# Down matrices asked for by the ScalarEngine, gate and up matrices by the SyncEngine, in a two-layer trunk with 64 experts a layer

## The reference

```python
def hier_moe(x, w_grp, b_grp, w_exp, b_exp, w_gate, w_up, w_down):
    # top-1 expert group of 8, then top-2 of its 8 experts; 64 experts in all
    ...
    def run_block(args):
        tok, e = args
        xb = x_pad[tok]
        h = jax.nn.silu(xb @ w_gate[e]) * (xb @ w_up[e])
        return h @ w_down[e]
    ...
    y = jnp.sum(y_assign.reshape(T, TOP_K, D).astype(jnp.float32) * weights[..., None], axis=1)
```

## Time and profile before

| | |
|---|---|
| median of 3 runs | 1505.33 us (1503.81 to 1505.48) |
| profiled execution, device time | 1503.91 us |
| its span | 1502.2 us |
| PE busy | 1259.2 us (84%) |
| DVE, ACT busy | 554.2 us (37%), 207.2 us (14%) |
| chain that ended last | PE 60%, DMA 36% |
| of that, transfers of `in_w_down` into `scratch` | 35% |
| matmuls of L1497 (down), in the chain | 11% |
| DMA queue q1 (SyncE) | 501.84 MB, 83.3% of 16 engines |
| DMA queue q10 (ScalarE) | 1.06 MB, 0.2% |

### The profile page before, as it was taken

The page is one execution under the profiler, slowest core; times in us unless marked ns, Lnnn a source line. Parts: engine busy times, 40 slices in busy tenths (PEclk is TensorE's granted clock), DMA queues, the critical chain, the costliest instruction groups (busy, mean ns, idle before and its releaser), DMA issues.

```text
span 1502.2 us, 20998 instructions
## 1 busy us (share of the span) xinstructions
PE 1259.2 (84%) x8621; PEld 690.0 (46%) x8621; DVE 554.2 (37%) x987; ACT 207.2 (14%) x413; POOL 27.9 (2%) x90
## 2 busy tenths in 40 slices
PE   9999999986774777579999999999677568757797
PEld 5665444742342434235466554456334325423354
DVE  6677775510110111111667677754111101101126
ACT  2322000310100000000212220012111000000011
POOL 2000000000000000000100000000000000000000
PEclk9999999997888889889999999999888879888899
DMA  9644558899999999999955255679999999999992
GB/s 314 230 172 150 174 211 332 318 426 426 427 427 425 425 425 426 428 427 416 330 192 204 97 204 168 230 301 355 426 427 426 427 426 424 426 426 428 426 408 87
DMA packets 110537, 503.85 MB, mean 335 GB/s; under 512 B 13042, under 2 KB 16132, under 8 KB 62468
## 3 DMA queue, kind: packets, MB, share of 16 engines
q1 hardware_dynamic: 109876, 501.84, 83.3%
q10 hardware_dynamic: 592, 1.06, 0.2%
HBM read 501.83 MB, written 1.05 MB: 335 GB/s over the span
## 4 chain that ended last, share of the span: by engine, by line
PE 60%; DMA 36%; issue 1%; SPq 1%; DVE 1%; ACT 0%; POOL 0%; DVEq 0%; POOLq 0%
DMA scratch<-in_w_down 35%; PE ps L852 20%; PE ps L1497 11%; PE ps L901 6%; PE ps L1448 5%; PE ps L805 4%; PE ps L1429 2%; PE ps L1507 2%; PE ps L1615 1%; PE ps L1344 1%; PE ps L825 1%; SPq L553 1%; PE ps L1316 0%; DMA ring<-in_w_in 0%; PE ps L1367 0%
## 5 line engine op out<-in xcount | busy, mean ns | idle before, releaser
L1497 PE MATMUL ps<-ring,pads 128*32 128x512 f32 x384 | 161.6, 784 | 199.2 <-DMA scratch<-in_w_down 199.2
L1497 PEld LDWEIGHTS ps<-ring,pads 128*32 128x32 f32 x384 | 33.9, 139 | 300.6 <-DMA scratch<-in_w_down 162.3
L1448 PE MATMUL ps<-scratch,pads 128*32 128x256 f32 x1792 | 171.6, 379 | 0.0
L1448 PE MATMUL ps<-ring,pads 128*32 128x256 f32 x2304 | 171.4, 379 | 0.0
L852 PE MATMUL ps<-ring,scratch 128*128 128x512 f32 x384 | 169.2, 592 | 0.0
L1497 PE MATMUL ps<-scratch,pads 128*32 128x512 f32 x512 | 161.6, 790 | 0.0
L2657 DVE COPY mats<-ps 128x512 f32<-128x512 f32 x32 | 22.1, 691 | 349.3 <-PE ps L1497 349.3
L1429 PEld LDWEIGHTS ps<-pads,xT 128*128 128x128 f32 x960 | 114.8, 197 | 25.3 <-issue 25.3
L1429 PE MATMUL ps<-pads,xT 128*128 128x128 f32 x960 | 116.0, 280 | 10.6 <-issue 10.6
L1507 PE MATMUL ps<-mats,pads 128*128 128x512 f32 x256 | 118.8, 606 | 0.0
L1448 PEld LDWEIGHTS ps<-scratch,pads 128*32 128x32 f32 x1792 | 89.3, 110 | 58.9 <-issue 17.6
(11 more groups left out here) (364 smaller groups left out, 1314.3 us busy)
## 6 DMA issues: line engine op xcount, KB each, us to landing
ring<-in_w_up SPq DMA_DIRECT2D x28, 2048.0 KB, 32.5
scratch<-in_w_down SPq DMA_DIRECT2D x28, 2048.0 KB, 23.0
scratch<-in_w_gate SPq DMA_DIRECT2D x28, 2048.0 KB, 30.4
ring<-in_w_in SPq DMA_DIRECT2D x48, 1024.0 KB, 7.1
ring<-in_w_gate SPq DMA_DIRECT2D x12, 3072.0 KB, 31.8
scratch<-in_w_up SPq DMA_DIRECT2D x14, 2048.0 KB, 31.9
ring<-in_w_down SPq DMA_DIRECT2D x14, 2048.0 KB, 27.0
scratch<-in_w_gate SPq DMA_DIRECT2D x22, 1024.0 KB, 14.5
```

Source lines behind the costliest of these rows:

```text
L1448: ins = mm(ps[32 * j:32 * j + 32, 2, i * 256:i * 256 + 256], xgT[:, k, 32 * j:32 * j + 32], w[j][:, k, :], start=(k == 0), stop=(k == K - 1))
L1497: ins = mm(ps[32 * j:32 * j + 32, n, :], hT[:, cc, 32 * j:32 * j + 32], w[j][:, cc, n * 512:n * 512 + 512], start=(cc == 0), stop=(cc == 1 ...
```

## The change

The high down matrices of most groups, and the low ones two groups ahead, are asked for by ScalarE: behind `take_down` of a turn it waits for `down_read` and issues high(s+1) and low(s+2). `down_read` is a new semaphore that PE raises with the second matmul of gate(s+1), that is, one matmul after the `ring_free` step that SyncE waited for before. SyncE keeps all gate and up matrices, the down matrices of groups 0 and 15, and around the sections' border low(1), low(8), high(8) and low(9). The slots and their order of reuse are as before. ScalarE's loop over turns now takes two groups a turn of the loop, and the last turns are written out.

```diff
@@ gate_up (TensorE)
+                                if i == 0 and k == 0 and j == 1 and not first:
+                                    ins.then_inc(down_read, 1)
@@ SyncE
                     with sp.Fori(first, PAIRS) as g:
                         for uu in range(2):
                             load_part(m + uu, GATE_UP, g)
-                            load_part(m + uu - 1, DOWN_HI, g)
-                            load_part(m + uu, DOWN_LO, g)
...
                 load_part(MID, DOWN_LO)
-                load_pairs(MID + 1)
-                load_part(GROUPS - 1, GATE)
-                load_part(GROUPS - 2, DOWN_HI)
-                load_part(GROUPS - 1, UP)
+                load_part(MID + 1, GATE_UP)
+                load_part(MID, DOWN_HI)
+                load_part(MID + 1, DOWN_LO)
+                load_part(MID + 2, GATE_UP)
+                load_pairs(MID + 1, 1)
+                load_part(GROUPS - 1, GATE_UP)
@@ ScalarE
+                def load_down(m, n, turn, g=None):
+
+                    act.wait_ge(down_read, turn)
+                    alone(act)
+                    s = m if m < MID else m + OVERG
+                    for n0, n1 in [run for run in PLAN[L]["runs"][s % 2] if n <= run[0] < n + 2]:
+                        q, e = MOE0 + 12 * s + n0, L * NE + 4 * m + n0 - 8
+                        src = a["w_down"][bass.ds(e if g is None else g * 8 + e, n1 - n0), :, :]
+                        act.dma_start(run_ap(PLAN[L]["slots"][q:q + n1 - n0]), src.rearrange("e (p k) n -> p e (k n)", k=2)).then_inc(
+                            landed[leader_of(L, s, n0)], 16)
...
+                    with act.Fori(0, pairs) as g:
+                        for uu in range(2):
+                            turn(g * 2 + (c0 + uu + 1))
+                            load_down(m0 + uu + 1, 10, g * 2 + (turns + uu + 1), g)
+                            load_down(m0 + uu + 2, 8, g * 2 + (turns + uu + 1), g)
+                    for i in range(2 * pairs, MID - 1):
+                        turn(c0 + i + 1)
+                        if m0 + i + 1 < (MID, GROUPS - 1)[s0 > 0]:
+                            load_down(m0 + i + 1, 10, turns + i + 1)
+                        if m0 + i + 2 < (MID, GROUPS - 1)[s0 > 0]:
+                            load_down(m0 + i + 2, 8, turns + i + 1)
```

More of the change, by code:

```diff
@@ L402, in build @@
         weights_ready = sem("weights_ready")
+        down_read = sem("down_matrices_read")
         def bank(p, i=0):
@@ L653, in _ @@
                 load_part(2, UP)
-                load_part(1, DOWN_HI)
-                load_part(2, DOWN_LO)
                 load_part(3, GATE_UP)
-                load_part(2, DOWN_HI)
-                load_part(3, DOWN_LO)
                 load_pairs(2, 1)
@@ L663, in _ @@
                 with sp.If(n_over > 0):
-                    load_part(MID - 1, DOWN_HI)
                     once(sp, "table_ready", L)
@@ L1839, in take_down, with turn @@
                     act.copy(ysb[:, 0:512], ps[:, 0, :]).then_inc(y_ready, 1)
+                def load_down(m, n, turn, g=None):
[7 more added lines that the diff above has]
+                            landed[leader_of(L, s, n0)], 16)
                 def section(s0):
-                    c0 = L * ALLG + s0
+                    c0, m0, pairs = L * ALLG + s0, s0 if s0 < MID else s0 - OVERG, PAIRS if s0 < MID else PAIRS - 1
+                    turns = 2 * (MID - 1) * L + (MID - 1 if s0 else 0)
                     take_gather(c0 + 1)
[L1844 to L1848, removed]
+                    def turn(c):
+                        take_silu(c)
+                        take_gather(c + 1)
+                        take_hidden(c)
+                        take_down(c)
+                    with act.Fori(0, pairs) as g:
[9 more added lines that the diff above has]
+                            load_down(m0 + i + 2, 8, turns + i + 1)
                     take_silu(c0 + MID)
```

## The result

| | before | changed |
|---|---|---|
| median | 1505.33 us, 7 runs (1502.56 to 1506.12) | 1508.89 us, 7 runs (1507.15 to 1511.38) |
| ratio | | 1.0030, interval of 95% 1.0019 to 1.0042 |
| span of the profiled execution | 1502.2 us | 1507.1 us |
| down(15) ends, layer 1 | 710.66 us | 712.59 us |
| down(15) ends, layer 2 | 1453.89 us | 1458.87 us |

The change costs 3.6 us of median, and 4.9 us between the two profiled executions. Single executions of one kernel lie about 4 us apart here, so the 4.9 is weaker evidence than the 3.6. All of those 4.9 us are there when the second down(15) ends (4.98). The first layer gives 1.93 of them, the second 3.05 (4.98 less 1.93).

The account below looks back on a forecast made before the run. Bytes at about 426 GB/s were taken to bound the MoEs, level with PE's path at each layer's end. +2.1 us a layer (+4.2) took 1503.91 to 1508.1; the median's 1.4 gave 1509.5 us, range 1500 to 1519.

Parts of the forecast that it names:

- Issues and waits, price 0: ScalarE's turns: 1 to 1.5 us of issues and the `down_read` wait fit its idle time before the SiLU; cost 0.
- The middle, price 0: Middle of the MoE: same bytes and rate, PE waits for up instead of high matrices; cost 0.
- The rate rivals: Transfers at the limit: two queues run 1% better (1501.2 us, chance 0.13) or 1% worse (1517.8 us, chance 0.10).
- The last wait: Layer's end: PE's last wait becomes that for up(14), ending at 679.3 us instead of high(13)'s at 669.47.
- a lag and then sharing: Queues: one that starts beside a full one loses some 2 us, then shares the rate.
- PE's path behind it: After up(14) lands: 32.5 us of PE work to the end of down(15), +1.1 us; slow-clock restart adds 2.1.
- The size, 2.1 a layer: Layer's end: net loss taken as +2.1 us from a span of -0.8 to +3.2, two layers +4.2.
- the place of high(14) between the two orders: Layer's end: whether high(14) is through before up(14) sets the loss; lag puts it a little later than an even share.
- Two level paths: Layer's end before the change: the bytes' path ends at 709.9 us and PE's at 710.7, about level.
- its lower end: Layer's end: high(14) not through before up(14), so last bytes alone set the end, 709.9 instead of 710.7: -0.8 us.
- the starved rival: Layer's end: service by order of arrival puts high(14) behind up(15), landing 698.7; +10.7 us a layer, 1526.7 us, chance 0.10.
- No change: Layer's end: high(14) and up(14) land about level or the restart is affordable; total -1.6 to +1.6, 1505.5 us, chance 0.25.

Follow-up runs that it names:

- e2: ScalarE asks for down matrices in each layer's first section only, the second as in the kernel before: 1504.80 us, ratio 1.0001 to the kernel before.
- e1: Changed kernel with high(14) given back to SyncE, between gate(15) and up(15): 1503.80 us, ratio 0.9995 to the kernel before.
- e7: Kernel before, with ScalarE asking for high(14) alone at the start of gate(14) and up(15) not held: 1504.73 us, ratio 1.0006.
- e8: The changed kernel run once more, unaltered, beside other runs: 1509.04 us, ratio 1.0031 to the kernel before.
- e10: Changed kernel with low matrices back on SyncE, plus 12 filler calls ahead of the wait for up(15): 1502.35 us, ratio 0.9988 to the kernel before.
- e4: Kernel before, SyncE alone, with up(15) asked for ahead of high(14): 1526.42 us, ratio 1.0146.
- e6: Changed kernel with the low matrices back on SyncE, ScalarE asking for the high ones alone: 1503.66 us, ratio 0.9994 to the kernel before.
- e9: Changed kernel with 30 filler calls between the gate and up halves of groups 10, 12 and 14: 1506.46 us, ratio 1.0013 to the kernel before.
- e11: Changed kernel with 30 filler calls between the halves of group 14 alone, last two PE turns written out: 1508.80 us, ratio 1.0036 to the kernel before.

## Why the prediction was right, point by point

Forecast 1509.5, measured 1508.89; forecast +4.2 us between profiled executions, measured +4.9.

**Issues and waits, price 0: right.** In one turn of the changed kernel, ScalarE's timeline has

```profile
638.25 0.40 ACTq L1846 DMA_DIRECT2D scratch<-in_w_down  x1
638.76 0.41 ACTq L1846 DMA_DIRECT2D ring<-in_w_down  x1
655.22 0.38 ACT L1828 ACTIVATE pads<-ps 128x256 f32<-128x256 f32 x1 [18.60 <-PE ps L1443]
```

two DMA instructions of 0.4 us, and 18.6 us of idle time ahead of the next SiLU. e2, where ScalarE issues the first section's, measured 1.0001.

**The middle, price 0: right, nearly.** Same bytes, 425 to 426 GB/s, and PE's waits moved from the high matrices to the up matrices, as forecast. High matrices land 14.2 us after their request (median of 26), in the 10 to 15 that were forecast. The rate rivals are out: a gain or loss of 1% would be 8.3 us, and e1, with all but one of ScalarE's requests of a layer, stands at 0.9995.

**The last wait: right, through a step that holds only in part.** Forecast 679.3, measured 678.41. It was worked out as if high(14) were through before the end of up(14). It wasn't: asked for at 667.74, it landed 13.7 us later, at 681.4, 3 us after up(14). Part of its bytes were still to come when up(14) landed. What q10 moved from 667.7 to 678.4 us (packets, MB) says how many:

```profile
q10 hardware_dynamic: 195, 1.60, 35.2%
```

1.60 of 2.10 MB came ahead, 3.8 us at 426 GB/s (e1 against the changed kernel gives 3.2, from two executions). The 0.50 MB behind are 1.2 us, near the 0.9 us by which up(14) was early; this part of high(14) no longer mattered, since PE wants it at 692.04. The prediction's picture of a lag and then sharing holds, with a longer lag: 3.5 us without a byte, not 2, and then half. 2 MB at half of 426 GB/s would take 9.8 us, and it took 13.7. Rows 6 and 7 could have given that number: SyncE's first load, asked for at 1.73 beside ScalarE's, begins at 5.0, 3.3 us later. ScalarE's own, with nothing beside it, was asked for at 0.78 and moves its first bytes at 1.8, so some 1 us of the 3.5 is there without a neighbour. What makes up the rest isn't shown. The Trainium skill ("DMA: Bandwidth & Descriptors", Queues, rings and completion order) has the engines go round the queues, a packet from each; that they share is borne out by e7 and by the halves above, the 3.5 us ahead of them are not in it.

**PE's path behind it: right.** 32.5 us plus the restart: 678.41 + 32.5 = 710.9, and 1.6 us of restart in layer 1 (5.14 less 3.5) make 712.5; measured 712.6. Layer 2 has 6.35 less 3.5, so 2.8. The mean is 2.2, the forecast was 2.1. The two layers differ by this: 3.05 - 1.93 = 1.1 us, and the restarts differ by 1.2.

**The size, 2.1 a layer: a compromise that fell right, in part by luck.** Measured 1.93 and 3.05, so 2.5 in the mean. By its own terms that is +1.1 for the order, less 0.9 for the bytes of high(14) still to come, and +2.2 for the restart; the prediction took 2.1 as a point between two ends and had no such sum. The term that moves it from execution to execution is the restart, 5.14 or 6.38 us behind a wait that ends at the same time (e8), not, as the prediction argued, the place of high(14) between the two orders.

**Two level paths: right, and the more useful part.** e1 and e10 end on the other one, last bytes at 709.9 and 709.5, and down(15) at 711.0 and 710.6. The prediction had 709.0 and 709.9: no run reached its lower end, and where the bytes set the end they gain nothing on the 710.7 of before. What the forecast's sum left out, though the starved rival has it, is that PE's lateness passes on to the bytes. The last pieces are asked for when down(14) is read, so with down(14) late they go out late. In layer 1, with down(14) 1.9 us late, the rate held (407 GB/s from 700.0 to 709.7, before 409). In layer 2, where down(14) starts at 1438.33 instead of 1433.33, it did not. The windows show it, first of the kernel before, then of the changed one, each up to about the landing of the last piece:

```profile
1441.00:1451.00 10.00, 9.68 (x95) 5.14 (x98) 1.03 (x2) 0.76 (x2) 0.00 (x0) 1.00 1.04 408
```

```profile
1446.00:1455.70 9.70, 9.38 (x94) 5.01 (x96) 1.03 (x2) 0.76 (x2) 0.00 (x0) 1.00 1.00 344
```

408 GB/s against 344, with no wait of PE for it: the transfers had become the shorter path, and the lost rate cost nothing. Why the rate fell isn't shown; the transfer engines' share is 1.00 over the window, and 0.885 for q1 in the lowest microsecond, 1447 to 1448.

**The rivals.** Starved: price right (e4, 1526.4 for 1526.7), condition wrong for two queues (e7). No change: this is the time of e1 and e6, so it was close, and hangs on one request in each layer. Rates: out.

## What to carry to other kernels

Where transfers ran at their limit, here at 425 to 426 GB/s, it made no difference which engine asked for them, as long as PE's waits only changed places (e2). Look at the last stretch of a section, where what lands last has uncovered work behind it, and count what comes in from the side ahead of the matrix that PE needs next. If requests are split over queues, keep the last ones in one queue, in the order in which they are needed: giving one request a layer back took away the whole loss here. By the traces a wait near the end costs its restart at half clock too, here 1.5 to 2.9 us; filler took that away where it left 0.9 us of idle time or none, not where it left 3.3 or 4.1. That filler shortens the time of a kernel isn't shown (e9, e11).

## What the runs showed of the hardware

**A DMA instruction that takes long on one engine doesn't hold up another engine's.** At the same time SyncE's DMA instructions take many microseconds, with some 45 us from a request to its landing, and ScalarE's take their usual 0.4. What holds SyncE's up isn't shown. The timelines of SyncE and of ScalarE in the changed kernel:

```profile
667.55 8.54 SPq L687 DMA_DIRECT2D ring<-in_w_down  x1
```

```profile
667.74 0.38 ACTq L1846 DMA_DIRECT2D scratch<-in_w_down  x1
```

**A transfer from the side is quick, but not at once.** 2 MB asked for by ScalarE beside SyncE's backlog landed after 13.7 to 15.1 us (changed kernel and e7), against the 23.3 us of the same request at the end of SyncE's own queue (e4) and the 9.8 us of an even share from the start. For the first 3.4 to 3.6 us q10 moved no byte (changed kernel, both layers, and e7 in both), and then half of the rate.

**The clock can fall after PE is at work again.** In e9 PE restarted at full clock behind 4.08 us of idle time (1.00 from 681.2 to 682.0), and the granted clock then fell (0.50 from 683 to 684). In e11 3.28 us of idle time were followed by a restart at 1.2 GHz, and 0.90 us by none.
